# First layer of a two-layer hybrid encoder: window attention and the preparation of the recurrence in one stage

## The reference, cut to what matters

```python
def even_mix(x, w_in, w_out, sink, rw, state=None):
    p = x @ w_in
    qa, ka, va, pb = split_cols(p, EVEN_SPLIT)
    ...
    oa = swa_sink_prompt(qa, ka, va, sink)            # sample: swa_sink_step, with the cache
    ob, new_shift, new_wkv = rwkv7(pb, shift, wkv, *rw)
    mix = jnp.concatenate([oa, ob], axis=-1) @ w_out

def softmax_with_sink(logits, sink):
    m = jnp.maximum(jnp.max(logits, -1, keepdims=True), sink)
    p = jnp.exp(logits - m)
    return p / (jnp.sum(p, -1, keepdims=True) + jnp.exp(sink - m))

def rwkv7(pb, shift_prev, S0, mu, w0, w_up, a0, a_up, g_up, k_k, k_a, r_k, lnx_g, lnx_b):
    xm = (pb + (prev - pb) * mu)                       # prev: pb one position earlier
    r, k, v, wl, al, gl = split_cols(xm, [B_WIDTH, B_WIDTH, B_WIDTH, W_LORA, A_LORA, G_LORA])
    w_log = -jax.nn.softplus(-(w0 + jnp.tanh(wl) @ w_up)) - 0.5
    decay = jnp.exp(-jnp.exp(w_log))
    a = jax.nn.sigmoid(a0 + al @ a_up)
    kk = heads(k * k_k)
    kk = kk * lax.rsqrt(jnp.sum(kk * kk, -1, keepdims=True) + 1e-12)
    k = k * (1.0 + (a - 1.0) * k_a)
    ...                                                # the recurrence over all positions
    bonus = jnp.sum(r * k * r_k, -1, keepdims=True) * v
```

## Time and profile before

| what | us |
|---|---|
| median of 3 runs (4169.97 to 4177.38) | 4172.51 |
| profiled execution, its own time | 4180.76 |
| span of the profiled execution | 4179.0 |
| projection of the first layer ends (last products) | 283.9 |
| attention, first block | 285.3 to 306.1 |
| attention, units | 306.1 to 420.2 |
| preparation of the recurrence | 420.2 to 536.8 |
| TensorE busy in the span | 3539.8 (85%) |
| DVE busy in the span | 2060.9 (49%) |

### The profile page before, as it was taken

One profiled execution on the slowest core, in us unless ns is written; L12 is line 12 of the kernel. 1 busy time (PEld: TensorE's weight loads), 2 busy tenths in 40 slices (PEclk: granted clock), 3 DMA queues, 4 the chain that ended last, 5 costly groups with the idle time before them and its releaser, 6 DMA issues. The chain is left out here.

```text
span 4179.0 us, 60716 instructions
## 1 busy us (share of the span) xinstructions
PE 3539.8 (85%) x26392; PEld 3208.5 (77%) x26411; DVE 2060.9 (49%) x2981; ACT 898.9 (22%) x1667; POOL 109.8 (3%) x51
## 2 busy tenths in 40 slices
PE   7978589858999999989977777776556899999996
PEld 6977289747999999979964445554434899999996
DVE  4415866566323232442127888898565542323235
ACT  1016411112101010120034444443223130101011
POOL 0010000001000000100000000000000100000001
PEclk9988599978999999989976788887677999999998
DMA  3110000111111111122210000001110111111111
GB/s 98 46 47 16 5 5 4 48 31 30 46 46 41 46 46 41 41 81 71 68 60 1 1 1 1 1 1 31 44 37 25 36 36 46 46 41 46 46 41 48
DMA packets 245727, 151.00 MB, mean 36 GB/s; under 512 B 33702, under 2 KB 239931, under 8 KB 244699
## 3 DMA queue, kind: packets, MB, share of 16 engines
q1 hardware_dynamic: 244504, 146.92, 11.9%
q10 hardware_dynamic: 962, 0.20, 0.0%
HBM read 127.08 MB, written 19.79 MB: 35 GB/s over the span
## 5 line engine op out<-in xcount | busy, mean ns | idle before, releaser
L239 PE MATMUL psum<-rounded,rounded 128*128 128x364 f32 x13464 | 2272.5, 330 | 66.3 <-DVE rounded L320 30.9
L239 PEld LDWEIGHTS psum<-rounded,rounded 128*128 128x128 f32 x13464 | 2256.2, 189 | 76.9 <-issue 65.0
L786 ACT ACTIVATE arena<-psum 128x1092 f32<-128x1092 f32 x64 | 69.4, 1084 | 1194.5 <-PE psum L239 1194.5
L800 DVE CAST rounded<-arena 128x1092 fp32r<-128x1092 f32 x64 | 46.7, 730 | 529.6 <-ACT arena L789 529.6
L225 DVE TENSOR_TENSOR rounded<-arena,rounded 128x1024 fp32r<-128x1024 f32 x187 | 276.7, 1479 | 6.5
L2111 PE MATMUL psum<-arena 128*128 128x128 f32 (+2 forms) x1424 | 242.8, 325 | 40.7 <-ACT arena L2175 40.5
L1554 PE MATMUL psum<-arena 64*64 64x64 f32 x8160 | 255.9, 220 | 23.9 <-POOL arena L1738 12.5
L1554 PEld LDWEIGHTS psum<-arena 64*64 64x64 f32 x8160 | 245.4, 135 | 35.4 <-DVE arena L1691 18.4
L2111 PEld LDWEIGHTS psum<-arena 128*128 128x128 f32 (+1 forms) x1424 | 218.7, 234 | 66.6 <-issue 39.7
L2095 PE MATMUL psum<-arena 128*128 128x128 f32 (+1 forms) x712 | 144.1, 340 | 136.1 <-ACT arena L2166 135.7
L223 DVE CAST rounded<-arena 128x1024 fp32r<-128x1024 f32 x187 | 128.6, 688 | 243.7 <-PE psum L239 229.4
(11 more groups left out here) (227 smaller groups left out, 2570.6 us busy)
## 6 DMA issues: line engine op xcount, KB each, us to landing
arena<-in_w_ff_up SPq DMA_DIRECT2D x128, 256.0 KB, 3.1
arena<-in_w_ff_down SPq DMA_DIRECT2D x128, 256.0 KB, 3.0
arena<-in_w_in_odd SPq DMA_DIRECT2D x44, 256.0 KB, 3.2
arena<-in_w_in_even SPq DMA_DIRECT2D x40, 256.0 KB, 3.5
x_kept<-arena SPq DMA_DIRECT2D x2, 4368.0 KB, 13.1
arena<-x_kept SPq DMA_DIRECT2D x2, 4368.0 KB, 13.1
arena<-in_x_prompt SPq DMA_DIRECT2D x1, 4096.0 KB, 19.8
arena<-in_cache_c_k SPq DMA_DIRECT2D x4, 1024.0 KB, 5.7
```

The lines of the kernel that those rows point to most:

```text
L239: last = nc.tensor.matmul(m.ps[:, out:out + TB], rounded(m, w)[:, k, :], rounded(m, x(k))[:, b * TB:(b + 1) * TB], start=(k == 0 and n == ...
```

## The change

`window_attention`'s two blocks and `rwkv_prepare` become one block, `window_and_prepare`. The edits:

- x is written by the first stage into tiles 12 to 19 of `m.p` (not yet in use), the projection reads it there and writes the low part to `m.x`; x is stored to DRAM from there during the projection, behind the first four weight loads, and tile 12 waits for the store. `join` is gone. The order of tiles is r and k, queries, v and gates, attention keys and values; the transpose of the shift's last columns comes after the last tile.
- The 24 gate products of all heads run ahead of the units, in pieces of 364 columns through two banks, each with its sigmoid. The sums of squares are taken per token: 36 products with the squares as stationary operand and two columns of ones give 72 columns (9 blocks of positions x 8 heads) on the partition of the token; one square root and one reciprocal on them. Each head's inverse norms are brought back to columns by 18 products with a broadcast column and the identity.
- The hardware loop over t is written out. Beside units of the attention stand parts of the recurrence: `gather` (running sum, new k, product for the bonus) after unit 0, 4, 8, 12, `norm_bonus` after 2, 6, 10, 14, `scale` after 3, 7, 11, 15, and ACT's three exponentials after 1, 5, 9, 13.
- Scores have one room of four (banks 0 and 1), moved probabilities one room of four; banks 2 and 3 serve the recurrence's parts.

```diff
-EVEN_TILES = list(range(4, 16)) + [18, 19, 16, 17, 0, 1, 2, 3]
+EVEN_TILES = list(range(4, 12)) + [0, 1, 2, 3] + list(range(12, 16)) + [18, 19, 16, 17]
...
+                if u == SLOTS - 1:
+                    sp.dma_start(io["x_kept"], given.rearrange("p k t -> p (k t)")).then_inc(kept, 16)
...
-                if u == shifts + 2:
+                if u == tiles - 1:
...
-            join(m, pool, m.joined)
...
+            def gather(h):
+                ended(dve, FA, h * 6 + 5)
+                if h:
+                    after(h - 1, "pc")
+                nc.vector.tensor_tensor_scan(cum, m.c("reset"), sg[:, h], 0.0, ALU.mult, ALU.add)\
+                    .then_inc(*BV.step("cum"))
...
+            for u in range(UNITS):
+                if u + 1 < UNITS:
+                    prepare(u + 1)
+                normalise(u)
+                if u + 1 in gathered:
+                    gather(gathered[u + 1])
+                if u + 1 in normed:
+                    norm_bonus(normed[u + 1])
+                if u + 1 in scaled:
+                    scale(scaled[u + 1])
...
+            def scores(u):
+                g = u % 2
+                ended(pe, AQ, u)
+                if u:
+                    pe.wait_ge(VP.sem, VP.done(u - 1, "logits3"))
...
+            def gate_products(h):
+                cols = slice(128 * h, 128 * h + 128)
+                for half in (0, 1):
+                    part = slice(64 * half, 64 * half + 64)
+                    for b in range(NB):
+                        n = h * 6 + half * 3 + b
+                        if n >= 2:
+                            ended(pe, FA, n - 2)
+                        nc.tensor.matmul(piece(n), wa_up[part, cols], p[part, 18, b * TB:(b + 1) * TB],
+                                         start=True, stop=True).then_inc(*one(FP))
+
+            def norm_sums():
+                ended(pe, FA, 23)
+                pe.wait_ge(FV.sem, FV.done(3, "square"))
+                for h in range(4):
+                    for t, (b, o) in enumerate(spots):
+                        last = nc.tensor.matmul(piece(0)[:, t * 8 + 2 * h:t * 8 + 2 * h + 2],
+                                                squared[:, h, b * TB + o:b * TB + o + 128], m.c("heads")[:, 0:128:64],
+                                                start=True, stop=True)
+                last.then_inc(sums_made, 1)
+
+            def norms_and_bonus(h):
+                pe.wait_ge(knormed, 1)
+                for b in range(NB):
+                    if b == 2:
+                        pe.wait_ge(BV.sem, BV.done(h, "kkn0"))
+                    elif h:
+                        pe.wait_ge(BV.sem, BV.done(h - 1, f"bon{b + 1}"))
+                    for t, (at, o) in enumerate(spots):
+                        if at == b:
+                            for odd in (0, 1):
+                                one_head = knorm[:, t, 2 * h + odd:2 * h + odd + 1].to_broadcast([128, 64])
+                                last = nc.tensor.matmul(piece(b)[64 * odd:64 * odd + 64, o:o + 128], one_head,
+                                                        m.c("ident"), start=True, stop=True)
+                    last.then_inc(*BP.step(f"inv{b}"))
+                pe.wait_ge(BV.sem, BV.done(h, "rkk"))
+                for b, free in enumerate(("kkn1", "kkn2", "bon0")):
+                    pe.wait_ge(BV.sem, BV.done(h, free))
+                    nc.tensor.matmul(piece(3 + b), m.c("heads"), tmp[:, b * TB:(b + 1) * TB], start=True, stop=True)\
+                        .then_inc(*BP.step(f"bon{b}"))
...
+            for u in range(UNITS):
+                turn_probs(u)
+                if u % 2 == 0 and u:
+                    turn_rows(u // 2 - 1)
+                if u + 2 < UNITS:
+                    scores(u + 2)
+                values(u)
+                if u + 1 in normed:
+                    norms_and_bonus(normed[u + 1])
```

More of the change, by code:

```diff
@@ L1100, in window_attention @@
-    names = ("a_scores", "a_probs_turned", "a_out", "a_rows_turned", "a_q", "a_probs_moved", "a_rows_moved")
-    PS, PT, PO, PU, AQ, AM, AU = (Steps(nc, n, [n]) for n in names)
-    VP = Steps(nc, "a_logits", [f"logits{h}" for h in range(4)] + ["max", "top", "low"])
-    VN = Steps(nc, "a_norm", ["sum", "inv", "norm"])
-    AE = Steps(nc, "a_exps", [f"exp{h}" for h in range(4)] + ["sink"])
-    kept = nc.alloc_semaphore("x_kept")
-    def one(steps):
-        return steps.step(steps.steps[0])
@@ L1110, in ended @@
-    def ended(engine, steps, unit):
-        engine.wait_ge(steps.sem, steps.done(unit, steps.steps[0]))
-    def kind(t):
-        return "first" if isinstance(t, int) and t == 0 else "sample" if isinstance(t, int) and t == NQ else "middle"
-    def keys(t):
-        return {"first": (128, 256), "sample": (0, 192), "middle": (0, 256)}[kind(t)]
-    def tiles(t):
-        return (1,) if kind(t) == "first" else (0, 1)
-    def rows_of(t, j):
-        return TS if kind(t) == "sample" and j == 1 else 128
@@ L1127, in window_attention @@
[L1127 to L1145 removed]
+            nc.gpsimd.memset(qz, 0.0).then_inc(cleared, 1)
@@ new lines, in _ @@
+            load(0)
+            nc.scalar.activation(p[0:64, 18, :], p[0:64, 18, :], ACT.Tanh).then_inc(gates, 1)
+            load(1)
+            for h in range(4):
+                for name, dst in (("w0", sg[:, h]), ("a0", m.a[:, h])):
+                    for b in range(NB):
+                        n = h * 6 + (0 if name == "w0" else 3) + b
+                        ended(act, FP, n)
+                        nc.scalar.activation(dst[:, b * TB:(b + 1) * TB], piece(n), ACT.Sigmoid,
+                                             bias=m.col(ROWS[name] + h)).then_inc(*one(FA))
@@ new lines, in norm_bonus @@
+            def norm_bonus(h):
+                for b in range(NB):
+                    part = slice(b * TB, b * TB + TB)
+                    dve.wait_ge(BP.sem, BP.done(h, f"inv{b}"))
+                    stt(out=m.kk[:, h, part], in0=m.kk[:, h, part], scalar=-1.0, in1=piece(b), op0=ALU.mult,
+                        op1=ALU.mult).then_inc(*BV.step(f"kkn{b}"))
+                for b in range(NB):
+                    part = slice(b * TB, b * TB + TB)
+                    dve.wait_ge(BP.sem, BP.done(h, f"bon{b}"))
+                    tt(m.bonus[h][:, part], piece(3 + b), v[:, h, part], ALU.mult).then_inc(*BV.step(f"bon{b}"))
+                after(h, "kkn2")
+                stt(out=m.a[:, h], in0=m.a[:, h], scalar=-1.0, in1=m.kk[:, h], op0=ALU.mult, op1=ALU.mult)\
+                    .then_inc(*BV.step("b"))
```

551 lines of the change are left out of this document (240 added, 311 removed).

## The result

| | median, us | range | runs | profiled execution, us | its span, us |
|---|---|---|---|---|---|
| before | 4172.51 | 4169.97 to 4179.61 | 7 | 4180.76 | 4179.0 |
| after | 4193.06 | 4179.58 to 4195.81 | 7 | 4193.12 | 4191.3 |

The ratio is 1.0041, with a 95% interval of 1.0029 to 1.0052: the change made the kernel slower by about 17 us (the two medians alone are 20.5 us apart). The forecast was no change, 4171.

The account below looks back on a forecast made before the run. No single engine but a closed chain was taken to bound the stage: scores wait for logits, values for scores, normalising for values. 2.0 + 43 + 190.4 + 14.5 + 0.5 = 250.4 against 251.5 gave 4171 us, range 4147 to 4205.

Parts of the forecast that it names:

- The sum for the stage: From the projection's tail to the recurrence: 2.0 + 43 + 190.4 + 14.5 + 0.5 = 250.4 us, against 251.5 before.
- the difference carries over: Whole kernel: the stage's -1.1 us passes unchanged to the median, giving 4171 us.
- The front: From the block's start to DVE's second logits: 3.9 + 25 + 9.2 + 5 = 43 us.
- norm sums: In the front, behind the last gate: 36 products, 72 records, 9.2 us, with ends of 4.6 and 14.6.
- The gates: In the front: 24 products in a row through two banks at half clock, 1.04 each, 25 us; ends 16 and 32.
- The units: Attention units with the recurrence's parts, a closed chain: 28.0 for four units, 47.6 with parts, 190.4 for four heads.
- norms and bonus: One of the recurrence's parts, per head: broadcasts 4.3, bonus products 1.8, last steps 1.9; 7.5 us less overlapping normalising.
- The removed wait: At the attention's start: the wait for GpSimd's clearing and rejoining of x, 19.56 us, goes.
- The first (the clock stays up): Faster rival, in the units: all at 5.7 us, 21 us less, 4150 (4161 with half of it); 17%.
- The second (gates at full clock): Faster rival, in the front: gates take 16 us instead of 25, 4162; 8%.
- The third: Slower rival, the clock stays down: units at 8.5, 46 us more, 4217, halfway 4192 likelier; 30%.
- The fourth (parts beside units): Faster rival: parts lie beside units, so DVE's work bounds; 170 us, 80 less, 4090; 3%.

Follow-up runs that it names:

- run 5: The changed kernel with 52 one-by-one-column products at the second layer's attention, second MLP's loop turning at instruction 251; 4176.73 us, 1.0001 of the kernel before.
- run 10: Two kernels: the changed kernel with 21 products (turn at 127), 4177.78 us, 1.0004; changed kernel with values ahead of scores and 52 products (turn at 251), 4154.17, 0.9947.
- run 1: The changed kernel again, unaltered; 4188.57 us, 1.0042 of the kernel before.
- run 2: The changed kernel with 64 unread one-column products ahead of everything, moving all TensorE code (loop turn at 42); 4205.63 us, 1.0074 of the kernel before.
- run 4: The changed kernel with TensorE's values of unit u (and norms and bonus) ahead of the scores of unit u+2; 4172.20 us, 0.9999 of the kernel before.
- run 6: The kernel before with 11 one-column products at the second layer's attention (turn at 42), 4179.38 us, 1.0011; with 16 (turn at 62), 4172.93, 0.9999.
- run 3: The kernel before with only the join removed (x kept in p, new order of tiles), its two stages apart; 4161.09 us, 0.9975 of the kernel before.
- run 7: The changed kernel with unread products keeping TensorE busy in the units, and 40 products moving the loop's turn to 251; 4163.24 us, 0.9974 of the kernel before.
- run 9: The changed kernel with values first, gates spread over units, loop's place mended, decays one unit later, own tile for head 1's bonus; 4136.64 us, 0.9907 of the kernel before.

## Why the prediction was wrong

**The sum for the stage held, the step behind it did not.** The sum was 250.4 us against 251.5. With the loop moved (run 5) the stage takes 1.1 + 52.1 + 184.4 + 15.1 = 252.7, 1.2 us over before, and the whole kernel 1.0001 of it. Single executions of this stage scatter around that: the recurrence started 5.9 us later than before in the kernel after, 1.4 later in run 1, and 7.4 earlier in run 10's changed kernel, whose gates ran at full clock for a part. The step that failed is "the difference carries over", with its premise that the rest of the program keeps its sums. The changed stage has more TensorE code, 1069 instructions as compiled (4 packets and 45), and everything behind it moved by that. The second MLP's loop, unedited, then turned at instruction 43 of a packet and not at 254, and lost 12 us. Of the 17 us of the result (1.0041) the trace accounts for these 12 and for 1 to 6 in the stage; what is left lies within the intervals.

The evidence for the place has both signs. At 42 or 43 all five profiled executions stood 3.1 to 5.1 us in a turn (after, and runs 1, 2, 4, and 11 products in 6); at 62, 127, 251 and 254 all others stood 1.1 or less. The first layer's MLP, a loop of the same length, narrows it further. The change moved its turn from 234 to 23, and in other runs it turned at 22, 31 and 71; at all of these it stood 0.5 to 1.1 us. Here are its two turns in run 10's changed kernel, at 23:

```profile
1410.38 89.90 PE L239 MATMUL psum<-rounded,rounded 128*128 128x364 f32 x537 [1.00 <-issue]
...
1603.81 96.41 PE L239 MATMUL psum<-rounded,rounded 128*128 128x364 f32 x576 [0.97 <-issue]
```

Thus neither the beginning of a packet nor a move as such is bad; of the places seen, 42 and 43 are. The loop's beginning moves along with its turn, so the runs do not tell which of the two matters. The code's packets show in the trace as a DMA queue of their own, of kind "instruction". In the 15 us around the first turn, the kernel before, then run 1:

```profile
q8 instruction: 3, 0.05, 1.4%
```

```profile
q8 instruction: 4, 0.07, 1.8%
```

All five executions at 42 or 43 have four there, at both turns; at every other place, in either MLP, two or three lie in such 15 us. The Trainium skill (Runtime: NRT & Kernel Launch, Instruction fetch mechanics) says that code is streamed in blocks of 16 KiB and that a taken branch to a block which isn't held waits for its fetch. The trace agrees with a wait at the turns, 0.5 us at least; why one packet more is fetched at 42 and 43, and why the wait is up to ten times as long there, these runs do not show.

**The front: 52.4 in place of 43, a mis-sized term.** Two prices were too low. The norm sums took 15.52 us for 72 records, 0.216 each, where I had 0.127 from the earlier trace rows and took that row for half clock. It was not: its stretch, kernel before,

```profile
1008.00:1012.00 4.00, 4.00 (x35) 0.91 1.10 291
```

has a granted clock of 0.91, while the norm sums ran at 0.50 (0.127 at 0.91 would be 0.23 at 0.50, an estimate from the two clocks). The upper bound that I gave, 14.6, was the nearer one. The gates took 28.13 us, 1.17 a product, where I had taken 1.04 between rows of 0.90 and 1.32. That two banks, with products of one half in a row, let less overlap is argued; no run isolates it. The other steps were 8.8, as forecast (3.9 + 5).

**The units: 47.6 a cycle forecast, 47.7 measured.** The chain is as described: scores wait for logits, DVE for values, half clock behind each gather and each scaling. But the agreement of the sums is luck in part. In the cycle shown the gather takes 7.2 us (7.1 forecast) and the scaling 4.9 (5.0), while norms and bonus take 5.9 (7.5): the parts are 1.6 us cheaper. The 18 broadcasts account for that, 2.39 us at a clock of 1.00 where I had 4.3; whether because pairs overlap or because their stationary operand has 64 columns, no run shows. The four units take 29.5 in place of 28.0, 1.5 us more, since the clock falls behind the bonus as well (0.50 in 423 to 425) and does not come back in the unit behind the scaling, which takes 9.1 us where 7.8 were forecast. Four cycles and their edges came to 187.7 (184.4 in run 5, where one cycle of 44.7 had regained the clock early) against 190.4. So an error of +9 in the front met -3 to -6 in the units: 7 us over the sum remained in the kernel after, 2 in run 5; there it is a nearly right sum with wrong terms.

**The other terms.** The tail of the projection, counted from its first products to the next block, was 1.0 to 2.0 us longer, forecast 2.0. The end was 15.1, forecast 15.0. The removed wait was worth 10 to 12 us by itself (run 3).

**The rivals.** The first (the clock stays up) did not come by itself; run 7 made it come, and it was worth 11 to 14 us of the 21 (173.8 against 184.4 and 187.7). The second (gates at full clock) came for a part of the gates in four of the eight profiled executions that have all 24 in the front, for 7 to 9 us. The third did not come as a whole: cycles were 44.7 to 48.0, in the one shown with one unit in four at half clock throughout. That the time, 4193, lies beside its halfway figure of 4192 is chance. The fourth (parts beside units) was rightly ruled out for the order as written, and one swap made it come in part: 164.2. The slower outcome that did come was none of the four.

## What to carry to other kernels

When a kernel becomes slower in a stretch that nobody edited, count the products in equal stretches of both traces and look at the turns of the loops there before you explain the edited stage: a handful of idle instructions ahead of the loop can be worth more than the edit. A price taken from a row is a price at that row's clock, so read the granted clock of its stretch along with it. And before work is merged beside a chain, find what closes the chain: here the swap on TensorE, the gates spread over the units and a later place for ACT's decays, with the loop's place mended, turned the same merger from no gain into 39 us.

## What the runs showed of the hardware

The place of this loop's code is worth 3 to 6 us at each turn: 5.10 and 4.72 us of standstill in the kernel after, 0.5 to 1.1 in every kernel with the loop elsewhere. In run 1 two fifths of the loss are the clock (11.7 us less 3.3 and 3.6), which falls to 0.50 in the pause; where seven products interrupted the pause, it stayed at 0.99 to 1.00 (run 6).

Identical gate products ran at two clocks. Where they began at 289.0 to 289.7 us (runs 4 and 7, both kernels of 10) the clock was 1.00 for their first 13 us or more, and all 24 took 18.7 to 21.4 us; where they began at 290.1 or later (after, runs 1, 2, 5) it was 0.50 throughout, 28.1 us. The Trainium skill (TensorE: Matmul & The Clock Gate, Part 1) has sustained matmuls release the throttle; 28 us of gates at 0.50, with TensorE busy throughout (28.13 us), disagree with it. The other four executions agree at first, with the clock back within 1 us of the first gate, and disagree later: it fell to 0.50 again while the gates ran on (4.00 us busy of 4.00 at 304 to 308 in run 4) or, in the last of them, the norm sums. The start alone does not decide it: the six gates in the front of run 9 began at 291.0 and had 1.00 in 293 to 295. What does I have not tried.
